# A decoder layer with expert lookup: the last ten query weight tiles in two transfers each

## The reference

```python
z = x @ w_in                         # pool | q | k | v | gate_pool | gate_attn
m = g_pool * (pool_out @ w_up_pool) + g_attn * (attn_out @ w_up_attn)
x = layer_norm(ALPHA * x + m @ w_out)
...
q  = (xb @ w_query)                  # 8 heads, 2 halves of 128
sc = einsum('thcd,hcnd->thcn', q, sub_keys)
top_s, top_i = top_k(sc, 16)         # then the best 16 of 16 x 16 pairs
u = expert_u[idx]                    # (tokens, 8, 16, 1024)
h = gelu(einsum('td,thkd->thk', xb, u))
y = einsum('thk,thkd->td', softmax(best_s) * h, expert_v[idx])
x = layer_norm(ALPHA * x + y)
```

## Time and profile before

| | |
|---|---|
| median of 3 runs | 3130.2 us |
| lowest and highest run | 3122.51 and 3130.29 us |
| span of the profiled execution | 3122.3 us |
| TensorE, VectorE, GpSimd busy | 84%, 74%, 40% of the span |
| DMA | 1259.45 MB, mean 403 GB/s |
| issues of the last ten query units | 2052.9 to 2179.1 us |

### The profile page before, as it was taken

The page is one execution under the profiler, slowest core; times in us unless marked ns, Lnnn a source line. Parts: engine busy times, 40 slices in busy tenths (PEclk is TensorE's granted clock), DMA queues, the critical chain, the costliest instruction groups (busy, mean ns, idle before and its releaser), DMA issues.

```text
span 3122.3 us, 30933 instructions
## 1 busy us (share of the span) xinstructions
PE 2634.2 (84%) x8060; PEld 1415.0 (45%) x8060; DVE 2305.6 (74%) x4994; ACT 958.4 (31%) x3103; POOL 1257.7 (40%) x1060
## 2 busy tenths in 40 slices
PE   8889989999998878999998878799977787666675
PEld 7766666555544434554444435434422232222222
DVE  2488777888866566888887666788988887666666
ACT  2133413333332223332345211433322323222222
POOL 0123334344443344343333434443544454454542
PEclk9899999999999999999999999999999999888989
DMA  9999999999999999999999999999999999999996
GB/s 291 258 417 404 376 416 417 419 420 419 419 420 417 416 417 366 420 419 420 401 400 369 417 419 420 421 420 408 412 421 421 421 421 421 421 422 422 422 422 285
DMA packets 204853, 1259.45 MB, mean 403 GB/s; under 512 B 31244, under 2 KB 34908, under 8 KB 69120
## 3 DMA queue, kind: packets, MB, share of 16 engines
q0 software_dynamic: 152064, 1107.36, 86.0%
q1 hardware_dynamic: 49856, 144.24, 12.7%
q10 hardware_dynamic: 2760, 5.88, 0.5%
HBM read 1251.72 MB, written 5.79 MB: 403 GB/s over the span
## 4 chain that ended last, share of the span: by engine, by line
DMA 43%; PE 29%; DVE 18%; issue 4%; ACT 3%; DVEq 1%; POOL 1%; ACTq 0%; POOLq 0%
DMA ring<-in_uv,idx 36%; PE acc L1119 13%; PE wide L1100 10%; DVE ring L1391 8%; DVE acc_v L1402 2%; DMA wring<-in_uv,idx 2%; PE wide L1315 2%; DMA bias<-in_uv,idx 1%; DMA wring<-in_w_q 1%; DVEq L1375 1%; PE wide L1288 1%; DMA wring<-in_w_a 1%; ACT diag L909 1%; POOL ring L864 1%; PE wide L1198 1%
## 5 line engine op out<-in xcount | busy, mean ns | idle before, releaser
L864 POOL DMA_INDIRECT ring<-in_uv,idx x910 | 1076.7, 1183 | 1567.7 <-PE acc L1119 1044.3
L1119 PE MATMUL acc<-ring,diag 128*128 128x512 f32 (+1 forms) x2820 | 1381.3, 631 | 283.8 <-ACT diag L909 261.2
L1391 DVE CUSTOM_DVE_ANT_0 ring<-ring,xb 128x1024 f32<-128x1024 f32 x910 | 1098.3, 1224 | 444.7 <-DMA ring<-in_uv,idx 409.3
L1119 PEld LDWEIGHTS acc<-ring,diag 128*128 128x128 f32 (+1 forms) x2820 | 542.8, 199 | 992.9 <-issue 975.5
L895 ACT ACTIVATE hgelu<-hdot 128x2 f32<-128x2 f32 x528 | 107.2, 203 | 1805.5 <-DVE hdot L1391 1805.2
L1100 PE MATMUL wide<-xm,wring 128*128 128x256 f32 (+5 forms) x2352 | 606.9, 407 | 18.2 <-DMA wring<-in_w_q 16.6
L1100 PEld LDWEIGHTS wide<-xm,wring 128*128 128x128 f32 x2352 | 426.1, 196 | 215.0 <-issue 106.3
L909 ACT ACTIVATE diag<-ident,hw 128x128 f32<-128x128 f32 x813 | 293.5, 396 | 42.8 <-issue 1.1
L1402 DVE SCALAR_TENSOR_TENSOR acc_v<-ring,hw,acc_v 128x1024 f32<-128x1024 f32 x205 | 263.4, 1285 | 24.6 <-ACT hw L898 4.2
L898 ACT ACTIVATE hw<-hgelu,gate 128x1 f32<-128x1 f32 x1056 | 253.9, 287 | 37.1 <-issue 0.7
L1315 PE MATMUL wide<-wring,big 128*128 128x256 f32 (+1 forms) x536 | 123.6, 381 | 3.6 <-DMA wring<-in_w_a 3.6
(11 more groups left out here) (242 smaller groups left out, 1967.3 us busy)
## 6 DMA issues: line engine op xcount, KB each, us to landing
wring<-in_w_a SPq DMA_DIRECT2D x141, 512.0 KB, 7.9
wring<-in_w_q SPq DMA_DIRECT2D x64, 576.0 KB, 8.1
ring<-in_uv,idx POOLq DMA_INDIRECT x910, 20.7
ring<-in_w_a SPq DMA_DIRECT2D x27, 512.0 KB, 8.3
xb<-in_x_rows SPq DMA_DIRECT2D x8, 512.0 KB, 14.2
out_y_prompt<-xb ACTq DMA_DIRECT2D x7, 512.0 KB, 8.2
att<-in_ln_g SPq DMA_DIRECT2D x4, 512.0 KB, 11.5
att<-in_ln_b SPq DMA_DIRECT2D x4, 512.0 KB, 14.8
```

The source lines that it names most:

```text
L864: pool.indirect_dma_start(slot(s), None, uv, bass.IndirectOffsetOnAxis(ap=idx[:, n % LISTS, j:j + 1], axis=0))\
L1119: k = mm(acc[0:width, c * 512:(c + 1) * 512], diag[:, r % DIAGS, 0:width], slot(s)[:, D + c * 512:D + (c + 1) * 512], start=(s == first), ...
L1391: V.tensor_tensor_reduce(u, u, x, 1.0, 0.0, ALU.mult, ALU.add, hdot[:, k, j:j + 1])\
```

## The change

In the last group, the query units from the seventh on (ten of sixteen) are loaded by two transfers: rows 0 to 119 and rows 120 to 127. Both add 16 to the buffer's semaphore, and `unit_in` waits for the larger count; `PARTS` counts the loads into that buffer that were made in two. Nothing else moves.

```diff
+UNEVEN = 6
+MOST = 120
+TWICE = [g == GROUPS - 1 and pos >= POS_QRY + UNEVEN for g, pos in UNIT_ORDER]
+PARTS = [sum(TWICE[m] for m in range(n + 1) if BUFFER[m] == k) for n, k in enumerate(BUFFER)]
...
+                if pos >= POS_QRY + UNEVEN and g == GROUPS - 1:
+                    dst, src = wring[:, BUFFER[u], :], w_q[pos - POS_QRY]
+                    sp.dma_start(dst[0:MOST], src[0:MOST]).then_inc(w_in_sem[BUFFER[u]], 16)
+                    sp.dma_start(dst[MOST:P], src[MOST:P]).then_inc(w_in_sem[BUFFER[u]], 16)
+                    return
...
-                pe.wait_ge(w_in_sem[BUFFER[u]], 16 * USES[u])
+                pe.wait_ge(w_in_sem[BUFFER[u]], 16 * (USES[u] + PARTS[u]))
```

## The result

The changed kernel takes 3155.6 us at the median of five runs (3147.6 to 3158.8) against 3130.2 (3122.5 to 3134.8). The ratio is 1.0078, 95% interval 1.0065 to 1.0092, or +24 us (20 to 29). Forecast were +0.8 us and a range up to 3136.

What follows compares the result with a forecast made beforehand. The prediction took the DMA engines, one of them alone for the last 9 to 10 us, to bound the kernel. It summed 3130.2 + 0 (issue) + 0 (waiting) + 0.8 (balance) = 3131.0 us, range 3120 to 3136.

Steps and rivals of the forecast that it cites:

- What bounds the kernel: Behind the last query tiles only the DMA engines set the pace, at 421 to 422 GB/s from 2240 to 3060 us.
- Issue and waiting at no cost: Ten more load issues (3.3 us) fit SP's idle time; TensorE's larger count has 16.7 us of slack: 0 us.
- Fifteen and eight engines: Per cut tile, 120 rows go over fifteen DMA engines, eight each, and 8 rows over eight engines, one each.
- the late engine among the first eight: The DMA engine working alone for the last 9 to 10 us also gets the extra rows: up to +1.75 us.
- rival A: Faster: the late DMA engine is the one left out by 120 rows, -8 to -10 us, 3120 to 3122; chance 0.14.
- The hint that placed the late engine: Near 36 us, a weight tile landing 3.5 us later was read as code loads hitting an engine that carries a plane.
- Balance over the DMA engines, the only part with a price: Ten cut tiles give eight engines ten more rows each, +1.75 us, partly absorbed: +0.8 us, between 0.3 and 1.75.
- Its nearest relative is the copy of the value cache, 8 planes: That copy, at 40 to 41 us, ran on eight engines; the even cut was carried over to 120 rows.
- Rival B: Slower: 120 rows go over fewer engines than fifteen, say eight with 15 rows each, +10 to +14 us; chance 0.07.
- Rivals C and D: C: no change, late engine unaffected or extra work absorbed, 3130, chance 0.11. D: tiles come late, +5 us, chance 0.02.
- slower 0.08: The chance the prediction gave to the changed kernel measuring slower, beside same 0.85 and faster 0.07.

Runs made afterwards that it cites:

- run 1: Changed kernel with the last ten query tiles cut along the columns (576 and 576), all 128 rows in both transfers: 1.0002 against the kernel before, 3131.3 us.
- runs 7 and 8: Kernel before plus six additional copies inside HBM near the end: on eight DMA engines 1.0023 (+7.2 us), on sixteen 1.0013 (+4.1 us).
- Run 2: Changed kernel with the ten tiles cut into 112 and 16 rows instead of 120 and 8: 1.0059 against the kernel before, +18 us.
- run 6: Changed kernel with the 120 and 8 row cut moved to the first group's last ten gate tiles, before any gather: 1.0003 against the kernel before.
- run 4: Changed kernel without the eight-row transfers, so only rows 0 to 119 of the ten tiles load: 1.0057 against the kernel before, +18 us.
- run 12: Changed kernel with the last ten query tiles loaded in eight transfers of 16 rows: 1.0120 against the kernel before, +38 us.
- run 3: Changed kernel with the ten tiles cut into 64 and 64 rows: 1.0070 against the kernel before, +22 us.

## Why the prediction was wrong, point by point

**What bounds the kernel:** right. The DMA engines set the pace, and bytes not moved while the tiles load (21 us worth) are found again in the time (+24 us).

**Issue and waiting at no cost:** right. Twice the transfers cut by columns cost 0.6 us (-1.9 to +3.4). The landings, given as 8 to 9 us, came some 2 to 3 us later than before, within the slack; the tiles of run 1 took as long, at no cost.

**Fifteen and eight engines; the late engine among the first eight; rival A unlikely:** right, by the 70 completion packets and runs 7 and 8. The hint that placed the late engine was luck in part: the tile that landed 3.5 us after the other ran beside the 32-row loads of `xT`, which may be what delayed it.

**The step that failed** is "Balance over the DMA engines, the only part with a price". I priced a transfer by how many bytes each engine gets, at 26.3 GB/s whatever rows the transfer takes in. That rate was the term at fault: it does not hold while a transfer over part of the rows runs. With 128 rows the engines serve tile and gathers at 25 to 26 GB/s each; with 120 rows in the same stretch at 17 to 18. Run 2 shows the loss without any imbalance, run 6 without gathers, and run 1 shows none with two transfers of all the rows. A hint of it stood in the trace: "Its nearest relative is the copy of the value cache, 8 planes" passed over the 32-row loads of `xT`, with 17.4 us to landing for 256 KB. The price of ten tiles was 24 us, not 0.8; the imbalance that I did price, and the small transfer, have at most the 6 us or so by which the change stands above runs 2 and 4, and the intervals nearly close that gap.

The Trainium skill has what I should have weighed. SBUF — State Buffer, "Door 1: The DMA port swizzle", says that DMA writes enter by 16 ports of eight rows each, that rows 0 to 31 reach only eight of them, and that rows 32 to 63 reach the same eight. DMA: Bandwidth & Descriptors, "The descriptor swizzle", says that a 128-row transfer gives each engine the rows of a port of its own, and sends other shapes to the section on how many engines are used; I read that section and not this one. An estimate from these pages, if an engine takes neighbouring rows otherwise: a cut transfer alone keeps eight of 16 ports, half the rate; beside gathers that take half of each engine's turns, those ports have 2 x 0.5 + 0.5 = 1.5 of what they carry, two thirds of the rate. The runs agree: 206 GB/s against 409 alone (run 6), 272 against 421 in the mix. (The half is an assumption. In the stretch above the tile's queue has 37.3% of the time, and with that it would be 1.37 and 0.73 of the rate, where 0.65 is measured.) For 16 rows at a time the same count gives four engines on a port, 2.5 times and 0.4 of the rate; run 12 shows 237 and 236 GB/s, 0.56, so the direction agrees and the size does not; that one engine's writes of several transfers overlap may be why, and was not tried. One thing does not follow from the count: by it, half of the ports stay free while 64 rows load, yet in run 3 all gather packets in the middle of the loads took longer, 0.49 us at the median against 0.31. Which rows an engine writes in a 120-row transfer no run shows; that is argued, and so is that it is the ports that are shared, and not another part of the on-chip memory or of HBM. What is shown is that the cut by rows does it.

**Rival B** named the right sign and half of the size (+10 to +14) by another mechanism, fewer engines, that did not happen. **Rivals C and D** did not happen either. The range ended at 3136, since I gave B and D together 0.09 (its line "slower 0.08" is a hundredth under that sum).

No version tried beats the kernel before; the best, the cut by columns, equals it.

## What to carry to other kernels

Cutting a load by rows is not free even if the bytes per DMA engine stay equal: 112 and 16, 64 and 64, or four times 32 rows of a 128-row tile each slowed all DMA traffic while they ran, by about a third at the worst. If a load must be cut, cut it by columns and keep all 128 rows; two halves of 2304 bytes a row is what was tried. And when a page of totals says that the DMA engines are busy, read GB/s beside the share: at a share of 1.00 with 272 GB/s, each packet took half as long again.

## What the runs showed of the hardware that I had not expected

Gathers on another queue slow down with the row-cut transfer: 26.2 to 16.9 GB/s per engine. Without gathers, 16 busy engines moved 206 GB/s where whole loads had 409, half as much. And one DMA engine ends 10 us after all others, about what 10 code loads of 1.02 us would cost it (that they cause it was not tested); 7.5 us more on eight engines cost 7.2 us because it is one of them.
